# RWKV heads: block-diagonal 128x128 matrices kept and multiplied as 64x64 blocks in quadrants of the array, masked products in three groups

## What is computed

```python
def rwkv7_recurrence(r, w, k, v, kk, a):
    def step(state, inp):
        r_t, w_t, k_t, v_t, kk_t, a_t = inp
        sa = jnp.einsum('bhvk,bhk->bhv', state, -kk_t)
        state = (state * w_t[:, :, None, :]
                 + sa[..., None] * (kk_t * a_t)[:, :, None, :]
                 + v_t[..., None] * k_t[:, :, None, :])
        return state, jnp.einsum('bhvk,bhk->bhv', state, r_t)
    _, y = lax.scan(step, state0, xs)      # over 512 tokens
y = head_group_norm(y, ln_w, ln_b) + bonus
out = y * g
```

## Time and profile before

| | |
|---|---|
| median of 3 runs | 3835.3 us (3829.93 to 3839.46) |
| profiled execution, its own time | 3837.58 us |
| its span, first to last instruction | 3835.7 us |
| PE busy | 3623.7 us (94%), 17279 matmul instructions |
| DVE, ACT, POOL busy | 52%, 32%, 14% |
| mean granted clock of TensorE | 0.975 |

### The profile page before, as it was taken

How to read it: one execution, slowest core, us unless ns; L and a number is a source line. 1 busy time by engine, 2 the same in 40 slices (tenths; PEclk the granted TensorE clock), 3 DMA queues, 4 the chain that set the end, 5 groups by cost and what they waited for, 6 DMA issues and landing times.

```text
span 3835.7 us, 44975 instructions
## 1 busy us (share of the span) xinstructions
PE 3623.7 (94%) x17279; PEld 2899.5 (76%) x17279; DVE 1989.1 (52%) x2747; ACT 1228.4 (32%) x1651; POOL 532.7 (14%) x398
## 2 busy tenths in 40 slices
PE   6999999899999999998998889999999899989998
PEld 5788888546888788876777768887888677767887
DVE  6555563464555554455566444446444433345445
ACT  3632232464322322233223132224222322233222
POOL 1220010010000221110132121112111100012111
PEclk8999999899999999999999999999999999989999
DMA  3233234001232232221200023232223222222231
GB/s 103 86 102 105 91 95 106 20 1 34 88 104 93 86 97 92 98 87 45 72 12 1 1 77 99 98 98 68 97 98 98 77 77 80 85 66 79 97 98 66
DMA packets 232517, 295.37 MB, mean 77 GB/s; under 512 B 21893, under 2 KB 201464, under 8 KB 232392
## 3 DMA queue, kind: packets, MB, share of 16 engines
q1 hardware_dynamic: 230864, 290.48, 24.0%
q0 software_dynamic: 1152, 3.05, 0.4%
q10 hardware_dynamic: 376, 0.12, 0.0%
HBM read 291.53 MB, written 2.10 MB: 77 GB/s over the span
## 4 chain that ended last, share of the span: by engine, by line
PE 82%; DVE 8%; ACT 4%; POOL 3%; issue 2%; POOLq 0%; ACTq 0%; DMA 0%; DVEq 0%
PE bank L304 23%; PE bank L306 22%; PE bank L305 22%; POOL tmp L636 1%; PE bank L333 1%; PE bank L335 1%; PE bank L334 1%; PE bank L2074 1%; ACT h_hi L550 1%; PE bank L2579 1%; PE bank L2110 1%; DVE x L681 1%; ACT whi L294 1%; DVE wlo L300 1%; DVE h_lo L665 1%
## 5 line engine op out<-in xcount | busy, mean ns | idle before, releaser
L304 PE MATMUL bank<-h_hi,whi 128*128 128x512 f32 x2800 | 1114.3, 398 | 57.2 <-DVE h_lo L665 38.2
L305 PE MATMUL bank<-h_lo,whi 128*128 128x512 f32 x2800 | 1101.8, 393 | 0.0
L306 PE MATMUL bank<-h_hi,wlo 128*128 128x512 f32 x2800 | 1101.4, 393 | 0.0
L294 ACT ACTIVATE whi<-raw 128x2048 fp32r<-128x2048 f32 x273 | 521.7, 1911 | 1400.6 <-PE bank L306 1346.1
L300 DVE TENSOR_TENSOR wlo<-raw,whi 128x2048 fp32r<-128x2048 f32 x273 | 631.9, 2315 | 435.1 <-ACT whi L294 434.8
L304 PEld LDWEIGHTS bank<-h_hi,whi 128*128 128x128 f32 x2800 | 533.8, 191 | 183.0 <-issue 64.0
L305 PEld LDWEIGHTS bank<-h_lo,whi 128*128 128x128 f32 x2800 | 533.7, 191 | 115.5 <-issue 4.9
L306 PEld LDWEIGHTS bank<-h_hi,wlo 128*128 128x128 f32 x2800 | 532.9, 190 | 112.6
L304 PE MATMUL bank<-u_hi,whi 128*128 128x512 f32 x1376 | 539.4, 392 | 27.0 <-DVE wlo L300 10.6
L305 PE MATMUL bank<-u_lo,whi 128*128 128x512 f32 x1376 | 538.2, 391 | 0.0
L306 PE MATMUL bank<-u_hi,wlo 128*128 128x512 f32 x1376 | 538.1, 391 | 0.0
(11 more groups left out here) (400 smaller groups left out, 3381.2 us busy)
## 6 DMA issues: line engine op xcount, KB each, us to landing
raw<-in_ffn_wgu SPq DMA_DIRECT2D x88, 1024.0 KB, 5.1
raw<-in_ffn_wd SPq DMA_DIRECT2D x44, 1024.0 KB, 4.9
raw<-in_mlp_w_up SPq DMA_DIRECT2D x32, 1024.0 KB, 5.7
raw<-in_mlp_w_down SPq DMA_DIRECT2D x32, 1024.0 KB, 4.9
raw<-in_odd_w_in SPq DMA_DIRECT2D x24, 1024.0 KB, 5.1
raw<-in_even_w_in SPq DMA_DIRECT2D x13, 1024.0 KB, 5.3
raw<-in_rg_w_in SPq DMA_DIRECT2D x8, 1024.0 KB, 5.8
raw<-in_odd_w_out SPq DMA_DIRECT2D x8, 1024.0 KB, 5.0
```

What stands on the lines that cost most here:

```text
L294: e.activation(whi[:, n % 2, :], raw[:, n % 2, :], ACT.Copy).then_inc(hi_ready, 1)
L304: pe.matmul(o, w_hi, r_hi, start=first, stop=False)
L305: pe.matmul(o, w_hi, r_lo, start=False, stop=False)
L306: return pe.matmul(o, w_lo, r_hi, start=False, stop=last)
```

## The change

All block-diagonal matrices are kept as their 64x64 blocks alone: chunk parity gives the partition half, so a head's four pairs of chunks take 256 columns instead of 512. Every product over them becomes one matmul per chunk, of 64 rows and 64 columns, in the quadrant given by the row half and the output half. Masks are cut to the same form once, by two POOL copies in `pool_even`.

- Masked products come in three groups with one PE signal each: (4), (0, 2), (1, 3). A group's heads lie in two banks, two products side by side in a bank. DVE makes eight masks of them instead of twelve, four with 512 columns and four with 256.
- U, rhs and D go by chunk; U has 256 columns, so ACT copies 256. Dm and DTm lie side by side, D's two products too, so one DVE add of 512 columns replaces two (of 256 columns at level 5).
- POOL's additions of the identity and its Gb products have 256 columns; its order is Dm0 Dm1 gb10 gb11.
- QT and Y1 go by chunk and head, into a bank for even and a bank for odd chunks, and their readers (DVE's QT add, ACT's Y1 copy) become two instructions each of 256 columns.
- Banks move: the scan writes its output to bank 5, N to banks 6 and 7, MT to 0 and 1. Waits move with them (yln before QT, N before rhs, MT before the first turn).

The diff, cut to its core:

```diff
+        m_half = tiles(o, 9, HD); o += 9 * HD
...
             for j in range(2):
+                e.tensor_copy(m_half[j * HD:j * HD + HD, :, :], m_full[j * HD:j * HD + HD, :, j * HD:j * HD + HD])
                 chain(e.tensor_copy(ident2[j * HD:j * HD + HD, :], ident[j * HD:j * HD + HD, j * HD:j * HD + HD]))
...
-        MORD = ((4, 0), (0, 0), (4, 1), (0, 1), (1, 0), (2, 0), (3, 0), (1, 1), (2, 1), (3, 1))
-        MBANK = (0, 2, 3, 4, 1)
+        MGRP = ((4,), (0, 2), (1, 3))
+        MBANK = ((0, 2), (3, 4), (1, 7))
...
+        def two(t):
+            return [[by_chunk(hz(h, t)[:, i * 4 * HD:i * 4 * HD + 4 * HD]) for h in HH] for i in range(2)]
+        (M0, M2), (M1, M3), (Dm, DTm), (Um, Gb) = (two(t) for t in range(4))
+        EE = (slice(0, HD), slice(HD, P))
...
+            for s, i in enumerate(MGRP[g]):
                 l_, r_ = ((be, al), (be, rt_of(p)), (kt_, al), (kt_, rt_of(p)), (al, be))[i]
...
-                for j in range(QT):
-                    q = slice(j * P, j * P + P)
-                    ins = pe.matmul(pbank[b][:, q], l_[r, q], r_[r, q], start=True, stop=True)
-                fr_pe.done(ins, f"m{i}{h}")
+                for c in range(8):
+                    q = slice(c * HD, c * HD + HD)
+                    o_ = slice((4 * s + c // 2) * HD, (4 * s + c // 2) * HD + HD)
+                    for h in HH:
+                        ins = pe.matmul(pbank[MBANK[g][h]][EE[c % 2], o_], l_[EE[h], q], r_[EE[h], q], start=True, stop=True)
+            fr_pe.done(ins, f"M{g}")
...
-                for j in range(QT):
-                    ins = pe.matmul(pbank[h][:, j * P:j * P + P], Gb[h][:, j, :], Dm[h][:, j, :], start=True, stop=True)
+                for c in range(8):
+                    e, j = EE[c % 2], c // 2
+                    ins = pe.matmul(pbank[2 * h][e, j * HD:j * HD + HD], Gb[h][e, j, :], Dm[h][e, j, :], start=True, stop=True)
                 bk_pe.done(ins, f"U{l}{h}")
...
-                for j in range(QT):
-                    q = slice(j * P, j * P + P)
-                    if l < 5:
-                        pe.matmul(pbank[2 + h][:, q], DTm[h][:, j, :], Um[h][:, j, :], start=True, stop=True)
-                    ins = pe.matmul(pbank[4 + h][:, q], Um[h][:, j, :], DTm[h][:, j, :], start=True, stop=True)
+                for i, (l_, r_) in enumerate(((DTm, Um), (Um, DTm))):
+                    if i == 0 and l == 5:
+                        continue
+                    for c in range(8):
+                        e, j = EE[c % 2], c // 2
+                        ins = pe.matmul(pbank[3 + h][e, (4 * i + j) * HD:(4 * i + j) * HD + HD], l_[h][e, j, :],
+                                        r_[h][e, j, :], start=True, stop=True)
                 bk_pe.done(ins, f"D{l}{h}")
...
-                for j in range(QT):
-                    ins = pe.matmul(pbank[2][h * HD:h * HD + HD, j * P:j * P + P], PM[h][:, j, HD:P],
-                                    MATS[h][1][:, j, :], start=True, stop=True)
+                for h in HH:
+                    ins = pe.matmul(pbank[(2, 4)[c % 2]][EE[h], c * HD:c * HD + HD], PM[h][e, j, HD:P], M1[h][e, j, :],
+                                    start=True, stop=True)
             bk_pe.done(ins, "QT")
...
-                        if l < 5:
-                            e.tensor_tensor(flat(Dm[h]), flat(Dm[h]), pbank[2 + h][:, :], ALU.add)
-                        do_bk(e, e.tensor_tensor(flat(DTm[h]), flat(DTm[h]), pbank[4 + h][:, :], ALU.add), f"D{l}{h}", p,
+                        w = slice(0 if l < 5 else 4 * HD, S)
+                        do_bk(e, e.tensor_tensor(hz(h, 2)[:, w], hz(h, 2)[:, w], pbank[3 + h][:, w], ALU.add), f"D{l}{h}", p,
                               False)
...
-            pe_mats(pe, 0, 0, 10)
+            for g in range(3):
+                pe_mats(pe, 0, g)
...
-                    pe_mats(pe, p + 1, 0, 2)
+                    pe_mats(pe, p + 1, 0)
                     pe_mean(pe, p)
-                    pe_mats(pe, p + 1, 2, 6)
+                    pe_mats(pe, p + 1, 1)
+                    pe_mats(pe, p + 1, 2)
                     pe_var(pe, p)
-                    pe_mats(pe, p + 1, 6, 10)
                     pe_rhs(pe, p + 1)
```

More of the change, by code:

```diff
@@ L2077, in pe_rhs @@
         def pe_rhs(pe, p):
+            fr_dve.wait(pe, "m021", p)
+            if p:
+                bk_act.wait(pe, "N", p - 1)
             for h in HH:
[L2079 to L2084 removed]
@@ L2085, in pe_rhs @@
-                fr_pe.done(ins, f"rhs{h}")
+                for c in range(8):
+                    o_ = slice((4 * h + c // 2) * HD, (4 * h + c // 2) * HD + HD)
+                    ins = pe.matmul(pbank[6][EE[c % 2], o_], M2[h][EE[c % 2], c // 2, :],
+                                    tokV[EE[c % 2], c // 2, EE[h]], start=True, stop=True)
+            fr_pe.done(ins, "rhs")
         def pe_level_u(pe, p, l):
@@ L2090, in pe_level_u @@
                     fr_pool.wait(pe, f"gb1{h}", p)
-                    fr_dve.wait(pe, "m31", p)
                 else:
@@ L2117, in pe_back @@
                 fr_pool.wait(pe, f"ra{h}", p)
-                for j in range(QT):
-                    ins = pe.matmul(pbank[h][:, j * P:j * P + P], DTm[h][:, j, :], RHS[h][:, j, :], start=True, stop=True)
+                for c in range(8):
+                    e, j = EE[c % 2], c // 2
+                    ins = pe.matmul(pbank[h][e, j * P:j * P + P], DTm[h][e, j, :], RHS[h][e, j, :], start=True, stop=True)
                 bk_pe.done(ins, f"P{h}")
@@ L2274, in act_rhs @@
         def act_rhs(e, p):
+            fr_pe.wait(e, "rhs", p)
             for h in HH:
-                fr_pe.wait(e, f"rhs{h}", p)
-                fr_act.done(e.activation(RHS[h][:, :, 0:HD], pbank[6 + h][:, 0:4 * HD].rearrange(
-                    "p (j n) -> p j n", j=QT), ACT.Copy), f"rhs{h}")
+                fr_act.done(e.activation(RHS[h][:, :, 0:HD], by_chunk(pbank[6][:, h * 4 * HD:h * 4 * HD + 4 * HD]), ACT.Copy),
+                            f"rhs{h}")
         def act_high(e, k):
@@ L2292, in rwkv_act @@
                         bk_pe.wait(e, f"U{l}{h}", p)
-                        bk_act.done(e.activation(flat(Um[h]), pbank[h][:, :], ACT.Copy), f"U{l}{h}")
+                        bk_act.done(e.activation(flat(Um[h]), pbank[2 * h][:, 0:4 * HD], ACT.Copy), f"U{l}{h}")
                     if p < 3:
@@ L2307, in rwkv_act @@
                     fr_dve.wait(e, "cp", p + 1)
-                bk_act.done(e.activation(YY, pbank[3][:, :], ACT.Copy), "Y1")
+                for j in range(2):
+                    ins = e.activation(odd_even(YY, j), odd_even(pbank[(3, 5)[j]][:, :], j), ACT.Copy)
+                bk_act.done(ins, "Y1")
                 bk_pe.wait(e, "N", p)
                 for j in range(2):
-                    ins = e.activation(*(m.rearrange("p (c j n) -> p j c n", j=2, n=HD)[:, j]
-                                         for m in (NN, pbank[(5, 7)[j]][:, :])), ACT.Copy)
+                    ins = e.activation(odd_even(NN, j), odd_even(pbank[6 + j][:, :], j), ACT.Copy)
                 bk_act.done(ins, "N")
@@ L2436, in rwkv_dve @@
             dve_bonus(e, 0)
-            dve_mats(e, 0, 0, 10)
+            for g in range(3):
+                dve_mats(e, 0, g)
             for p in range(4):
@@ L2465, in rwkv_dve @@
                 bk_pe.wait(e, "QT", p)
-                do_bk(e, e.tensor_tensor(QTt, pbank[2][:, :], rt_of(p), ALU.add), "QT", p, False)
+                for j in range(2):
+                    ins = e.tensor_tensor(odd_even(QTt, j), odd_even(pbank[(2, 4)[j]][:, :], j), odd_even(rt_of(p), j), ALU.add)
+                do_bk(e, ins, "QT", p, False)
                 if p < 3:
```

141 lines of the change are left out of this document (68 added, 73 removed).

## The result

The changed kernel takes 3768.7 us (median of 4 runs, 3760.44 to 3769.65) against 3832.6 for the kernel before in the same comparison (4 runs); the ratio is 0.9826, 95% interval 0.9806 to 0.9846. That is 1.7% less, 63.9 us by the medians, where 63 were predicted. The profiled execution is 3768.28 us long (span 3766.5), 69.3 less than the profiled one before.

What follows compares the result with a forecast made beforehand. PE work was taken to bound the kernel (82% of the chain that ended last). Savings less POOL's copies summed to 75.1 us, less 12 for the clock left 63: median 3772.3 us from 3835.3, range 3752 to 3826.

Steps and rivals of the forecast that it cites:

- pair 0, masked products to kk: First head pair, start of masked products to PE's kk product: 6.9-7.3 us instead of 11.94, saving 4.6.
- into pairs 1 and 2, bonus to kk: From bonus product to the next pair's kk product: 11.2 us instead of 17.23, saving 6.0, twice: 12.0.
- into the last pair, bonus to first D: No kk product here, so PE goes to U after rhs; D starts at 8.4 us instead of 15.8, saving 7.4.
- levels, kk to copy, at the full clock: From kk product to the copy of PM[1]: 22.0 us against 32.95, saving 11.0, three times 33.0.
- last pair, first D to copy: Last pair's levels, no other work: PM[1] copied 17.2 us after the first D, against 28.7, saving 11.5.
- last steps, last pair: PM[1] copy to first scan step, set by PE and its handovers: 5.0 us against 7.9, saving 2.9.
- POOL's copies: Two mask copies added in pool_even, not hidden, 0.7 us each: 1.4 us lost.
- clock: PE's granted clock falls after waits: two falls for each of three pairs, 2 us each, costing 12 us.
- A: Rival, 33%: clock low for a large part of the stage; some 30 us saved, 3805 (3790 to 3830).
- C: Rival, 6%: slower, with low clock from first level to last scan over all four pairs; 3855 us in all.
- B: Rival, 6%: products in diagonal quadrants do not overlap, as both row halves write one bank; levels keep PE time, 3803 us.
- D: Rival, 5%: work moves but ends do not, as front work on DVE and ACT sets every level; 3830 to 3840 us.

Runs made afterwards that it cites:

- the filled run: Changed kernel with PE products nobody reads put into PE's waits before the kk product and before the first scan step; ratio to the kernel before 0.9824, stage 286.2 us.
- the order of the chunks: Changed kernel with the 64x64 products of U and D issued for the four even chunks first, then the odd; ratio to the kernel before 0.9856, stage 306.8 us.

## Why the prediction was right, step by step

| step | predicted | measured |
|---|---|---|
| pair 0, masked products to kk | 4.6 | 11.94 -> 6.73: 5.2 |
| into pairs 1 and 2, bonus to kk | 12.0 | 17.23 -> 11.44 twice: 11.6 |
| into the last pair, bonus to first D | 7.4 | 15.77 -> 8.17: 7.6 |
| levels, kk to copy, at the full clock | 33.0 | 32.95 -> 22.25, three times: 32.1 |
| last pair, first D to copy | 11.5 | 28.70 -> 17.2: 11.5 |
| last steps, three pairs | 5.1 | 7.89 -> 5.8, 6.57, 5.8: 5.5 |
| last steps, last pair | 2.9 | 7.89 -> 6.53: 1.4 |
| POOL's copies | -1.4 | 1.31 at the wait, 0.6 on the path |
| clock | -12 | 1.4 + 2.5 + 1.5 = 5.4 lost, 1.2 gained in the last scan: -4.2 |
| sum | 63 | 70 by marks, 69.7 by the stage |

The share of the levels, 32.1 and 11.5, is shown by the run that issues their products twice; the share of the transitions between pairs is read from marks, and the doubled masked products show that PE's time is on the path there. The steps on PE's rates held because each was read from a row of the right kind: U's 16 instructions take 0.47 us, a group of masked products 0.015 an instruction, the period of a level is 3.42. DVE on 256 columns took 0.41 (0.37 taken), POOL 0.73 (0.7), front_3 3.1 (0.42 + 1.63 + 1.04). That 3.1 was taken too is luck in its parts: the first instruction fell from 1.29, to 0.42, and the scan, which took 1.2 before, took 1.63 beside a POOL product of 1.62. The lower bound of 2.4 for it did not appear, as the slowing moved from two of the instructions to the scan.

Three steps were off, and their errors partly cancel. *The clock* was charged 12 us for six falls of 2; there were three before the last pair, for 5.4, and the fall in the last pair's scan, which the earlier trace rows show before the change too, became cheaper. The mechanism was as predicted (the falls stood before D, behind the waits of 3.6 us for the tail, and behind N), their number was not: behind N there was one in pair 0 and in the last pair only. The charge took 7.8 us too much. *The last pair's last steps* were to take 5.0; they took 6.53 because of the stand in N, and 4.95 without it. I had the rate of four-quadrant products from MT's burst of 32 weight loads and did not ask how long PE's supply of instructions lasts at that rate. *POOL's copies* cost what was said where they stand, but less than half of it further on, presumably because the wait is followed by other waits with slack.

The rivals: A (a large part of the stage at the low clock) did not occur: the four falls take some 20 us of it, and the page's clock digits show no slice below 9 there; what the falls cost is known from the filled run. C (slower) needed the low clock nearly throughout and fell with it. B is refuted by the order of the chunks and D by the doubled products. As to B, the Trainium skill's rule (TensorEngine Tiling (Array Packing), § Restrictions and Gotchas), that different row tiles may not use one PSUM bank at once, did not hold in this form: U and D of the changed kernel write one bank from both row halves, to different output halves, at 0.029 us an instruction.

The medians give 63.9 us, the two profiled executions 69.3 and the stage 69.7; the interval of the ratio, 59 to 74, holds them all. So the agreement of 63 with 63.9 to within 1 us is luck. The stage says that the sum was 6.7 too low: the clock's charge by 7.8, the other way 1.5 for the last pair's last steps.

## What to carry to other kernels

Blocks of 64x64 in alternating quadrants are worth their saved time only where PE is on the chain; in a loop of small products and adds, compare PE's part of the period with what stays behind it, and test it by issuing the products twice. Where bursts of such products are long, count PE's instructions: a block of 256 that PE works off faster than its successor is brought becomes a stand that no semaphore explains. And a long wait of one engine (24 us here) says little; look for the first later point at which another engine stands because of it.

## What the runs showed of the hardware

- PE's instructions come in blocks of 256 (16 KB packets in the instruction queue, 12 more of them for 3072 more instructions). Where PE stood at the end of a block, it went on 2.6 to 4.3 us after entering that block; the longest (4.28) had weight transfers of over 300 GB/s running until the packet started. All 28 stands over 0.55 us inside bursts of small products, in ten runs, lie at one remainder modulo 256.
- 64x64x64 products in float32: 0.015 us an instruction over four quadrants, 0.029 over the two diagonal ones in turn, 0.058 within one quadrant. Two products in a row in one quadrant cost nothing more (0.029); with four in a row the average is 0.042, as the next quadrant's first instructions start beside the last three.
- After waits of PE of 2 to 4 us, and of 5.3 in the projections, the granted clock of the changed kernel fell to its lower level for 3.4 or 6.8 us at a time; with idle products in the waits it stayed at 1.00 in all four places of the RWKV part, and with the wait in the projections gone it stayed at 1.00 there. The length of the wait alone does not decide it: before the scan of pair 0 it was 2.10 us and the clock fell, in pair 2 2.15 and it did not.
